# Second layer's experts: two shared down products moved between routed groups, table products moved among shared gate and up products

## What is computed

```
def moe_ffn(xf, w_router, b_router, we_gate, we_up, we_down, ws_gate, ws_up, ws_down):
    top_idx, top_w = route(xf, w_router, b_router)
    routed = routed_experts(xf, top_idx, top_w, we_gate, we_up, we_down)
    shared = (jax.nn.silu(xf @ ws_gate) * (xf @ ws_up)) @ ws_down
    return routed + shared
```

## Time and profile before

| | us |
|---|---|
| median of 3 executions | 2620.27 (2620.18 to 2622.15) |
| the profiled execution | 2621.41 |
| its span, first to last instruction | 2619.6 |
| PE busy | 2352.7 (90%) |
| DVE busy | 831.7 (32%) |
| ACT busy | 654.7 (25%) |
| POOL busy | 278.7 (11%) |

### The profile page before, as it was taken

The page is one execution under the profiler, slowest core; times in us unless marked ns, Lnnn a source line. Parts: engine busy times, 40 slices in busy tenths (PEclk is TensorE's granted clock), DMA queues, the critical chain, the costliest instruction groups (busy, mean ns, idle before and its releaser), DMA issues. The chain is left out here.

```text
span 2619.6 us, 34138 instructions
## 1 busy us (share of the span) xinstructions
PE 2352.7 (90%) x13484; PEld 1243.6 (47%) x13484; DVE 831.7 (32%) x1715; ACT 654.7 (25%) x1413; POOL 278.7 (11%) x260
## 2 busy tenths in 40 slices
PE   6999999799899999999993879998889998989874
PEld 3544555475544333333331768886644333333322
DVE  2332556526511010100104945555462000000005
ACT  1111444421011212121212444444311111111111
POOL 1000000031011111111110000000211111111100
PEclk9999999999999999999997989999999999989997
DMA  8566200112479999999985611100347999999967
GB/s 330 194 225 210 97 1 1 69 65 109 187 295 358 375 378 405 390 369 379 382 317 210 260 37 37 37 25 1 141 181 309 415 419 419 420 418 407 411 277 312
DMA packets 122205, 646.55 MB, mean 247 GB/s; under 512 B 18648, under 2 KB 29912, under 8 KB 60352
## 3 DMA queue, kind: packets, MB, share of 16 engines
q1 hardware_dynamic: 92512, 556.21, 54.4%
q0 software_dynamic: 29248, 87.12, 8.5%
q10 hardware_dynamic: 288, 1.05, 0.1%
HBM read 604.38 MB, written 57.75 MB: 253 GB/s over the span
## 5 line engine op out<-in xcount | busy, mean ns | idle before, releaser
L1564 PE MATMUL E_psG<-E_gu,E_xT 128*32 128x512 f32 (+2 forms) x2544 | 531.8, 613 | 44.7 <-DMA E_gu<-in_we_up_dram 29.1
L1858 DVE TENSOR_TENSOR E_hh<-E_sil,E_psG 128x256 f32<-128x256 f32 x96 | 40.4, 421 | 1082.6 <-ACT E_sil L1697 1082.6
L1564 PEld LDWEIGHTS E_psG<-E_gu,E_xT 128*32 128x32 f32 (+2 forms) x2544 | 157.0, 122 | 288.8 <-issue 281.8
L1578 PE MATMUL E_psY<-E_dn,E_hT 128*32 128x512 f32 (+2 forms) x1272 | 261.9, 596 | 1.5 <-ACT E_hT L1700 1.5
L1564 PE MATMUL E_psG<-fT,E_xT 128*32 128x512 f32 (+2 forms) x704 | 239.2, 623 | 3.5 <-DMA E_gu<-in_we_up_dram 3.1
L1564 PE MATMUL E_psG<-o,E_xT 128*32 128x512 f32 (+2 forms) x736 | 225.3, 611 | 6.0 <-DMA E_gu<-in_we_up_dram 6.0
L1697 ACT ACTIVATE E_sil<-E_psG 128x256 f32<-128x256 f32 x96 | 36.9, 384 | 658.3 <-PE E_psG L1564 658.3
L1439 POOL DMA_INDIRECT y_d<-E_yb,E_sca x94 | 94.3, 1004 | 984.4 <-ACT E_yb L1703 984.4
L1703 ACT ACTIVATE E_yb<-E_psY,E_wgt 128x1024 f32<-128x1024 f32 x96 | 107.0, 1115 | 289.4 <-PE E_psY L1578 289.4
L1564 PE MATMUL E_psG<-raw,E_xT 128*32 128x512 f32 (+2 forms) x464 | 148.3, 594 | 1.2 <-DVE E_xT L1855 1.2
L1557 PEld LDWEIGHTS E_psX<-cst,E_tmp 128*128 128x128 f32 x768 | 94.2, 193 | 73.3 <-issue 73.3
(11 more groups left out here) (396 smaller groups left out, 3724.0 us busy)
## 6 DMA issues: line engine op xcount, KB each, us to landing
E_gu<-in_we_gate_dram SPq DMA_DIRECT2D x70, 1024.0 KB, 11.2
E_gu<-in_we_up_dram SPq DMA_DIRECT2D x70, 1024.0 KB, 15.9
E_dn<-in_we_down_dram SPq DMA_DIRECT2D x70, 1024.0 KB, 15.0
h<-in_w_ada_dram SPq DMA_DIRECT2D x40, 1024.0 KB, 4.8
o<-in_we_gate_dram SPq DMA_DIRECT2D x24, 1024.0 KB, 12.1
o<-in_we_up_dram SPq DMA_DIRECT2D x24, 1024.0 KB, 15.6
o<-in_we_down_dram SPq DMA_DIRECT2D x24, 1024.0 KB, 15.1
I_ring<-y_d SPq DMA_DIRECT2D x24, 1024.0 KB, 7.1
```

What stands on the lines that cost most here:

```text
L1564: ins = nc.tensor.matmul(psG[c:c + n, 0].rearrange("p (v f) -> p v f", v=2), xT[:, k, c:c + n], slots[s][0][:, :, k], start=(k == 0), stop ...
L1578: ins = nc.tensor.matmul(psY[c:c + w, n], hT[:, j, k, c:c + w], slots[s][1][:, k, n * 512:(n + 1) * 512], start=(k == 0), stop=(k == KF - 1))
L1858: V.tensor_tensor(hh[:], sil[:], psG[:, 0, FF:2 * FF], ALU.mult).then_inc(done, 1)
```

## The change

In the second layer only:

- TensorE's table products are put between parts of the third shared gate and up product: table 0 after its first quarter, table 1 after three quarters, tables 2 and 3 behind it. `shared_down(0)` moves behind the tables.
- Only the shared down products of tiles 0 and 1 (`LATER` = 2) stay ahead of the extra block. Those of tiles 2 and 3 go between the first routed groups: `later_turned` and `later_down`, in the passes of groups 0 and 1, through banks that are free there (`psG[:, 1]` and `psS`) and a new tile `hTl`. ScalarE's copy (`later_hidden`) and VectorE's additions (`add_later`, two of 512 columns) move with them.
- The slots change roles: the extra block uses slot 3 (`XS`), and the slot in `o` is number 4 (`SHARED`), so that expert 3 is loaded behind the extra block and expert 4 takes the shared expert's place.
- SyncE issues the down weights of slots 4 and 5 when all four shared down products are done, and this wait now stands behind the loads up to gate and up of expert 7 and down of expert 6.

The core of the diff:

```diff
@@ -1265,14 +1265,16 @@
...
-            SHARED, XB = 3, 3
+            XB = 3
+            SHARED, XS = (3, XSLOT) if nt > NL else (4, 3)
+            LATER = nt if nt > NL else 2
...
@@ -1343,6 +1345,10 @@
...
+                if LATER < nt:
+                    hTl = T("hTl", [P, KF, P])
+                    psL = [psG[:, 1], psS[:]]
+                    turnedL = psG[:, 1, 0:KF * P].rearrange("p (k n) -> p k n", k=KF)
...
@@ -1372,38 +1378,39 @@
...
                         sp.wait_ge(s_ctl, 1)
                         e = expert_of(sp, NE)
-                        load_gate_up(sp, l, slots[XSLOT], e, s_xg)
-                        load_down(sp, l, slots[XSLOT], e, s_xd)
-                        for p in range(2):
+                        load_gate_up(sp, l, slots[XS], e, s_xg)
+                        load_down(sp, l, slots[XS], e, s_xd)
+                        for p in range(3):
                             e = expert_of(sp, plan.rank[p])
+                            if p == 2 and nt > NL:
+                                sp.wait_ge(s_sgu, nt - 1)
                             load_gate_up(sp, l, slots[p], e, s_lgu[p])
                             load_down(sp, l, slots[p], e, s_ld[p])
-                        e = expert_of(sp, plan.rank[2])
-                        if nt > NL:
-                            sp.wait_ge(s_sgu, nt - 1)
-                        load_gate_up(sp, l, slots[2], e, s_lgu[2])
-                        load_down(sp, l, slots[2], e, s_ld[2])
                         e = expert_of(sp, plan.rank[SHARED])
                         sp.wait_ge(s_sgu, nt - 1)
                         load_gate_up(sp, l, slots[SHARED], e, s_lgu[SHARED])
                         if ring > RING:
                             more = expert_of(sp, plan.rank[RING])
                             load_gate_up(sp, l, slots[RING], more, s_lgu[RING])
-                            sp.wait_ge(s_sht, nt)
-                            load_down(sp, l, slots[RING], more, s_ld[RING])
-                        sp.wait_ge(s_sdn, nt)
-                        load_down(sp, l, slots[SHARED], e, s_ld[SHARED])
+                        if LATER == nt:
+                            sp.wait_ge(s_sdn, nt)
+                            load_down(sp, l, slots[SHARED], e, s_ld[SHARED])
+                        held_back = e
                         m = extras_of(sp)
                         with sp.Fori(0, m) as x:
                             e = expert_of(sp, x + (NE + 1))
                             sp.wait_ge(e_gu, x + 1)
                             sp.sem_inc(s_bear, 1)
-                            load_gate_up(sp, l, slots[XSLOT], e, s_xg)
+                            load_gate_up(sp, l, slots[XS], e, s_xg)
                             sp.wait_ge(e_dn, x + 1)
                             sp.sem_inc(s_bear, 1)
-                            load_down(sp, l, slots[XSLOT], e, s_xd)
+                            load_down(sp, l, slots[XS], e, s_xd)
                         before = None
                         for p in range(ring, NE):
+                            if p == ring + 2 and LATER < nt:
+                                sp.wait_ge(s_sdn, nt)
+                                load_down(sp, l, slots[SHARED], held_back, s_ld[SHARED])
+                                load_down(sp, l, slots[RING], more, s_ld[RING])
                             s, e = p % ring, expert_of(sp, plan.rank[p])
                             sp.wait_ge(s_gu, plan.last[p - ring] + 1)
...
@@ -1530,6 +1537,25 @@
...
+                        def later_turned(t):
+                            pe.wait_ge(s_hm, t + 1)
+                            pe.wait_ge(s_shT, t)
+                            pe.wait_ge(s_gc, nt - 1)
+                            if t > LATER:
+                                pe.wait_ge(s_ha, t)
+                            x = up[:, t % UPS].rearrange("q (p k) -> q k p", k=KF)
+                            for k in range(KF):
+                                ins = nc.tensor.transpose(turnedL[:, k], x[:, k], ident)
+                            ins.then_inc(s_sht, 1)
+
+                        def later_down(t):
+                            pe.wait_ge(s_shT, t + 1)
+                            pe.wait_ge(s_tbl, 1)
+                            for b in range(2):
+                                for k in range(KF):
+                                    ins = nc.tensor.matmul(psL[b], hTl[:, k], wd[:, k, b * 512:(b + 1) * 512], start=(k == 0), stop=(k == KF - 1))
+                            ins.then_inc(s_sdn, 1)
...
@@ -1631,20 +1657,22 @@
...
                             place_caps()
                             place_extras()
-                            for t in range(1, nt):
-                                shared_gate_up(t)
+                            shared_gate_up(1)
+                            shared_gate_up(2)
+                            shared_gate_up(3, 0, 2)
                             table(0)
+                            shared_gate_up(3, 2, 6)
                             table(1)
-                            shared_down(0)
+                            shared_gate_up(3, 6, KD)
                             table(2)
                             table(3)
-                            for t in range(1, nt):
+                            for t in range(LATER):
                                 shared_down(t)

-                        whole = [(0, P, XSLOT)]
+                        whole = [(0, P, XS)]
                         pe.wait_ge(s_ctl, 1)
                         xs = extras_of(pe)
-                        pe.wait_ge(s_ha, nt - 1)
+                        pe.wait_ge(s_ha, LATER - 1)
...
@@ -1656,7 +1684,7 @@
...
                             pe.wait_ge(e_hT, x + 1)
                             pe.wait_ge(s_xd, 16 * x + 16)
-                            pe.wait_ge(s_ha, nt)
+                            pe.wait_ge(s_ha, LATER)
...
@@ -1667,10 +1695,16 @@
                             pe.wait_ge(s_xv, g + 1)
                             landed(g, 0)
                             gate_up(parts_of(g), s_gu)
+                            if LATER + g < nt and g == 0:
+                                later_turned(LATER)
                             if g + 1 < NGR:
                                 rows_turned(g + 1)
+                            if LATER + g < nt and g > 0:
+                                later_turned(LATER + g)
                             if g >= 1:
                                 down_of(g - 1)
+                            if LATER + g < nt:
+                                later_down(LATER + g)
                         pe.wait_ge(s_mul, NGR)
                         turn_hidden(s_ht)
...
@@ -1726,8 +1760,14 @@
...
                             for t in range(1, nt):
                                 copies(t)
-                            for t in range(nt):
+                            for t in range(LATER):
                                 shared_hidden(t)
+
+                        def later_hidden(t):
+                            act.wait_ge(s_sht, t + 1)
+                            if t > LATER:
+                                act.wait_ge(s_sdn, t)
+                            nc.scalar.activation(hTl[:], turnedL, ACT.Copy).then_inc(s_shT, 1)
...
@@ -1748,9 +1788,13 @@
...
                             act.wait_ge(s_gu, g + 1)
                             silu(s_sil)
+                            if LATER + g < nt and g == 0:
+                                later_hidden(LATER)
                             if g + 1 < NGR:
                                 act.wait_ge(s_tx, g + 2)
                                 rows(s_xa)
+                            if LATER + g < nt and g > 0:
+                                later_hidden(LATER + g)
                             if g >= 1:
                                 out_of(g - 1)
...
@@ -1788,7 +1832,7 @@
...
                         V.tensor_copy(ctl_i[0:1, 0:NE], psN[0:1, 5 * NE:6 * NE])
-                        next_rank = 5 * NE + plan.rank[XSLOT]
+                        next_rank = 5 * NE + plan.rank[XS]
...
@@ -1848,8 +1892,13 @@
...
                         V.tensor_scalar(gat[:], rowi[:], 3, None, ALU.arith_shift_right)
                         link(V.tensor_copy(wgt[:], psS[:, TBL:2 * TBL]), s_tbl)
-                        for t in range(nt // 2 if nt > NL else 0, nt):
+                        for t in range(nt // 2 if nt > NL else 0, LATER):
                             add_shared(t)
+
+                        def add_later(t):
+                            dve.wait_ge(s_sdn, t + 1)
+                            V.tensor_tensor(h[:, t, 0:512], h[:, t, 0:512], psL[0], ALU.add)
+                            V.tensor_tensor(h[:, t, 512:1024], h[:, t, 512:1024], psL[1], ALU.add).then_inc(s_ha, 1)

                         def rows(done):
...
@@ -1871,6 +1920,8 @@
...
                                 dve.wait_ge(s_tx, g + 2)
                                 rows(s_xv)
```

(10 more changed lines are left out.)

## The result

| | before | after |
|---|---|---|
| median of 12 executions, us | 2620.7 | 2624.97 (2622.5 to 2631.28) |
| after / before | | 1.0029, 95% interval 1.0019 to 1.0040 |
| span of the profiled execution, us | 2619.6 | 2622.9 |
| from the last rank product to the end of the last down product, us | 613.3 | 622.2 |

What follows compares the result with a forecast made beforehand. Weight transfers were taken to bound the second layer's experts. A 4.3 us head start against 5.0 us of owed loads gave +0.7, taken as +0.5 us: 2621.9 us profiled, 2620.8 us median, range 2615.0 to 2625.5.

Steps and rivals of the forecast that it cites:

- The tables' order and VectorE's operands: Tables among third shared gate and up: operands ready in time, no stall, routing table out 4.5 us earlier.
- The four gate and up loads, costed at nothing: Two gate and up loads behind the third shared product, issued at 1968.1 instead of 1963.1: no cost, at most 5 us.
- The gather's landing, 6.4 to 7.5 us: Extra block's gathered rows, issued at 1975.4: land 6.4 to 7.5 us later, within bounds of 6.4 and 11.4.
- The stall, 0.5 us: TensorE's wait for gathered rows at the extra block: 0.5 us, leaving it 8.2 us ahead.
- The rival of the late gather: At the extra block: rows land after 11.4 us, TensorE waits 4.5, clock costs 2.6; +6.6 us, 2627.4 us; chance 0.12.
- the 0.5 of the sum: End of the experts and everything behind it: +0.5 us, taken from a transfer sum of +0.7 us.
- The transfers, -4.3 + 5.0: Queue at the seventh expert's down load: 4.3 us ahead, two held loads owed costing 5.0 us; +0.7 us.
- A wait for the gathered rows above 2 us: Sign of being wrong: TensorE waits over 2 us for the extra block's rows.
- a queue still busy at 2024: Sign of being wrong; right would be an empty queue at about 2021 to 2025 us.
- TensorE's first wait for weights: In the routed groups: at 2148 us as before if right; 5 us later or absent if wrong.
- The range: Whole kernel: 2615.0 to 2625.5 us, chance 0.80 within; 0.13 slower, 0.07 faster.
- The rivals of faster: Whole kernel: held loads free, 2616.0 us, chance 0.13; TensorE the bound after all, 2619.4 us, chance 0.07.

Runs made afterwards that it cites:

- e1: Kernel before with only the table products moved among parts of the third shared gate and up product; all four shared down products ahead of the extra block: 1.0001.
- e2: Changed kernel with all four shared down products ahead of the extra block again, the down loads of slots 4 and 5 still held: ratio to before 1.0022.
- e4: Changed kernel with three products of no use on TensorE between the second shared down product and the wait for the gathered rows: ratio to before 1.0012.
- e6: Changed kernel, both later down products between first and second group's gate and up, held loads right behind them, before the seventh expert's down load: 1.0026 to before.
- e8: The changed kernel run again as it is, on the chip of three other runs: ratio to before 1.0021.
- e10: Changed kernel with slot 5's held load issued once the last shared rows are turned, ahead of the seventh expert's down load; gather still late: 1.0021 to before.
- e5: Changed kernel with the table products back in their old places, the rest of the change kept: ratio to before 1.0025.
- e3: Changed kernel with SyncE waiting for the extra block's gathered rows before issuing the four gate and up loads of slots 4 and 5: 1.0001 to before.
- e7: Changed kernel, four gate and up loads waiting for the gathered rows, later down products and held loads ahead of the seventh expert's down load: 1.0000 to before.
- e9: Changed kernel, four gate and up loads waiting for the gathered rows, slot 5's held load issued ahead of the seventh expert's down load: 0.9996 to before, 2614.74 us.

## Why the prediction was wrong, point by point

- *The bound.* Right. The stage ends when the weights have been moved, and bytes missing at 150 us were missing at the last wait for weights, within 2.4 us in all kernels. (My reading of the slices was one off: the full rate stands from slice 32, and TensorE's waits for weights before were 50.1 us in thirteen waits; 38.2 us in ten are those for `E_gu` alone.)
- *The tables' order and VectorE's operands.* Right: the tables ended at 34.3 (34.2 forecast), and there was no stall of TensorE.
- *The four gate and up loads, costed at nothing.* Right for the queue, which did not run dry; wrong for what it overlooked. They were issued 16.7 us before the gather in the old kernel and 7.0 us before it in the new one (1960.67 to 1967.71), and the gather had to share the queue with them.
- *The gather's landing, 6.4 to 7.5 us: the step that failed.* It took 9.4 us. I wrote that the queue was full in the old kernel too. It was full when that gather was issued, and nearly drained when it landed: 16 loads and three gathers end at 1986, by my own account of it, and it landed at 1986.3. The seven profiles with the gather some 4 us earlier, in a full queue, had 9.2 to 9.5 us (changed, e1, e2, e4, e6, e8, e10), e5 with it nearly as late as before 6.9, and e3 and e7 with an empty queue 4.4. Seen from the rank product, all nine with the four loads ahead of the gather landed at 44.7 to 47.0, though it was issued anywhere from 35.5 to 40.6, and the queue drained just then (before, 307 GB/s and then 170 from 1986 on; after, 377 and then 98 from 1978 on). I had the bounds right, 6.4 to 11.4, and took the end that was nearest in kind rather than the one whose queue looked alike.
- *The stall, 0.5 us.* It was 2.64 us, and 2.9 us more at the low clock: 5.6 us of TensorE's head start. The rival of the late gather was what happened, at 0.12 by my chances. It was priced at 6.6 us over the time before plus the 0.5 of the sum, 7.1 in all; the ratio is 7.6 us and the medians 4.3. Its point of decision, a landing later than 6.9 us, was right, and its parts were 4.5 us of wait and 2.6 for the clock, where 2.64 and 2.9 came.
- *The transfers, -4.3 + 5.0.* The mechanism and both sizes held where the gather was in time (e3: 0.4 us behind, +0.7 forecast). e2 measured the 5.0 alone at 4.3, with 0.1 us of difference in TensorE's line. With the gather late the head start was gone and the loads were owed: 5.7 us behind.
- *The signs.* A wait for the gathered rows above 2 us and a queue still busy at 2024 (84.7, where the share was 1.00) were named as signs of being wrong, and both came. TensorE's first wait for weights was to come when it had come before, at 208.8; it came at 200.0, and at 194.6 in e3, which lost nothing. So it tells of the new order of the loads, not of the loss.
- *The range.* The median of the changed kernel, 2624.97, lies inside 2615.0 to 2625.5, at its end; but I had put 0.80 on no difference that can be measured, and the ratio shows 0.29% slower.
- *The rivals of faster.* None showed itself. Transfer time was not spare after 100 us, since what was behind at 150 us stayed behind.

The Trainium skill (DMA: Bandwidth & Descriptors, Queues, rings and completion order) has each engine take turns between its queues packet by packet. I had drawn from it that the gather would stay near the lower figure. What I made of it was wrong: the gather took 9.2 to 9.5 us beside the loads against 4.4 us in an empty queue. No run shows the turns themselves, nor whether the gather took its turns beside the loads or stood mostly behind those issued ahead of it.

**What stays open.** How the gather and the loads share the queue, as said above. Why the clock fell after three of four waits of 2.5 to 2.6 us: in these three it had also come back up late behind the rank product (granted 0.54 to 0.66 in the 2 us from 4 us on, 1.00 in e8), and e4, which kept it with its products of no use, is of the late kind too (0.67). That speaks for these products, in one profile. How large the loss is, between the 4.3 us of the medians and the 7.6 us of the ratio (e8: 6.2 and 5.5). And whether e9 is faster than the kernel before.

## What to carry to other kernels

Where a stage waits for its transfers, moving work from before a point to after it only helps if buffers come free earlier for good: count the bytes served up to the moment from which the queue stays full, and count with them every load that the moved work keeps waiting. A small transfer on which the compute engine will depend is dear in a full queue; see what is queued until it *lands*, not when it is issued, and issue the large loads that nobody needs yet behind it.

## What the runs showed of the hardware

- The extra block's gather, rows of 4 KB, took 9.2 to 9.5 us from issue to landing beside a full queue of 1 MB loads (seven profiles), 6.4 and 6.9 us in a queue that drained meanwhile (before, e5), and 4.4 us in one that was empty at its issue (e3, e7).
- After a wait of 2.5 to 2.6 us of TensorE the extra block's gate and up ran partly at 1.2 GHz in three profiles (9.5 to 9.8 us) and at 2.4 GHz in a fourth (7.13 us). With three products of no use in the wait (e4) it was 7.13 us as well, in one profile.
- The last group's gate and up took 10.03 us after a wait of 3.88 us (changed; 0.50 granted from 2536 to 2539), 8.78 after 2.19 us (e8) and 7.09 after 2.35 us (e3).
- All that lies ahead of the last rank product took 1929.3 to 1939.4 us in the twelve profiles, and the kernels are the same up to there. A difference of 5 us in a stage is better read from a point just before the stage than from the whole time.
